# Moving weight sums from VectorE to GpSimd, and two more projections to seven products

## The reference, cut to what matters

```python
proj = x @ w_in[l]                       # 1024 x 6400, cut into 12 pieces:
# a_q 512, a_k 128, a_v 128, b_h 512, b_b 512, b_c 512, c_q 512, c_k 512, c_v 512, g_a, g_b, g_c 1024 each
y_a = sliding_window_attention(a_q, a_k, a_v, sinks)   # 8 heads of 64, 2 key/value heads, window 128
y_b = b_b * conv3(b_c * b_h)
y_c = moba_attention(c_q, c_k, c_v)      # 8 heads of 64; with one block of 256 it is causal attention
merged = sigmoid(g_a)*(y_a @ w_br_a) + sigmoid(g_b)*(y_b @ w_br_b) + sigmoid(g_c)*(y_c @ w_br_c)
x = layer_norm(ALPHA*x + merged @ w_out)
x = layer_norm(ALPHA*x + (silu(x @ w_gate) * (x @ w_up)) @ w_down)    # hidden width 2816
```

## Time and profile before

| | |
|---|---|
| median of 3 runs | 2504.95 us |
| profiled execution | 2509.21 us |
| its span, first to last instruction | 2507.3 us |
| TensorE busy | 2206.5 us, 88% |
| VectorE busy | 1181.2 us, 47% |
| ScalarE busy | 366.2 us, 15% |
| GpSimd busy | 38.5 us, 2% |
| mean granted TensorE clock | 0.96 |

### The profile page before, as it was taken

How to read it: one execution, slowest core, us unless ns; L and a number is a source line. 1 busy time by engine, 2 the same in 40 slices (tenths; PEclk the granted TensorE clock), 3 DMA queues, 4 the chain that set the end, 5 groups by cost and what they waited for, 6 DMA issues and landing times.

```text
span 2507.3 us, 43433 instructions
## 1 busy us (share of the span) xinstructions
PE 2206.5 (88%) x19414; PEld 1567.8 (63%) x19414; DVE 1181.2 (47%) x2135; ACT 366.2 (15%) x818; POOL 38.5 (2%) x69
## 2 busy tenths in 40 slices
PE   8999999999999999999999988888799986555564
PEld 7898699488987984746545645454488643232322
DVE  6776477687755875935533221222435631111111
ACT  1121000012210000234521000000201520000000
POOL 0000000000000010000000000000000000000000
PEclk9999999999999999999998999999999998888877
DMA  8655755476558564511327999999921189999996
GB/s 318 223 167 200 242 183 213 154 252 236 168 185 268 169 222 162 199 45 36 118 111 331 418 427 426 426 427 425 377 103 34 71 339 425 427 426 428 427 427 282
DMA packets 168411, 659.15 MB, mean 263 GB/s; under 512 B 8326, under 2 KB 55938, under 8 KB 143522
## 3 DMA queue, kind: packets, MB, share of 16 engines
q1 hardware_dynamic: 162544, 639.66, 65.5%
q0 software_dynamic: 5312, 16.57, 2.1%
q10 hardware_dynamic: 370, 0.15, 0.0%
HBM read 655.12 MB, written 1.23 MB: 262 GB/s over the span
## 4 chain that ended last, share of the span: by engine, by line
PE 61%; DMA 29%; DVE 7%; ACT 2%; issue 1%; DVEq 0%; SPq 0%; ACTq 0%
PE psum L2291 21%; DMA ring<-in_moe_w_up 10%; DMA ring<-in_moe_w_gate 9%; DMA ring<-in_moe_w_down 9%; PE psum L789 5%; PE psum L2459 4%; PE psum L538 4%; PE psum L2236 3%; PE psum L2349 3%; PE psum L715 3%; PE psum L603 2%; PE psum L601 2%; PE psum L806 2%; PE psum L2467 1%; PE psum L2312 1%; PE psum L859 1%
## 5 line engine op out<-in xcount | busy, mean ns | idle before, releaser
L789 PE MATMUL psum<-ring,arena 128*32 128x256 f32 x5888 | 382.7, 416 | 161.8 <-DMA ring<-in_moe_w_up 87.3
L789 PEld LDWEIGHTS psum<-ring,arena 128*32 128x32 f32 x5888 | 207.8, 118 | 333.5 <-issue 138.3
L806 PE MATMUL psum<-ring,lnp 128*32 128x256 f32 x3072 | 193.9, 407 | 71.0 <-DMA ring<-in_moe_w_down 66.5
L1649 DVE TENSOR_TENSOR arena<-psum,spare 32x512 f32<-32x512 f32 (+1 forms) x128 | 70.9, 554 | 363.5 <-PE psum L806 362.2
L806 PEld LDWEIGHTS psum<-ring,lnp 128*32 128x32 f32 x3072 | 104.3, 116 | 158.4 <-DMA ring<-in_moe_w_down 50.5
L1638 DVE TENSOR_TENSOR lnp<-arena,psum 128x512 f32<-128x512 f32 (+1 forms) x32 | 26.1, 815 | 331.3 <-PE psum L789 331.3
L2291 PE MATMUL psum<-ht,ring 128*128 128x128 f32 x1408 | 168.2, 279 | 4.4 <-DMA ring<-in_w_in 3.4
L2291 PEld LDWEIGHTS psum<-ht,ring 128*128 128x128 f32 x1408 | 163.3, 195 | 8.4 <-issue 8.4
L538 PE MATMUL psum<-ring,ht 128*128 128x512 f32 x320 | 140.6, 595 | 0.0
L1096 ACT ACTIVATE arena<-psum 128x512 f32<-128x512 f32 (+1 forms) x32 | 15.7, 490 | 674.0 <-PE psum L789 674.0
L2693 DVE SCALAR_TENSOR_TENSOR spare<-ring,arena,spare 128x512 f32<-128x512 f32 x168 | 113.4, 743 | 0.0
(11 more groups left out here) (517 smaller groups left out, 3175.0 us busy)
## 6 DMA issues: line engine op xcount, KB each, us to landing
ring<-in_moe_w_down SPq DMA_DIRECT2D x64, 2048.0 KB
ring<-in_moe_w_gate SPq DMA_DIRECT2D x62, 2048.0 KB
ring<-in_moe_w_up SPq DMA_DIRECT2D x60, 2048.0 KB
ring<-in_w_in SPq DMA_DIRECT2D x52, 1024.0 KB
ring<-in_ada_w SPq DMA_DIRECT2D x48, 1024.0 KB
ring<-in_w_ffn_gate SPq DMA_DIRECT2D x22, 1024.0 KB
ring<-in_w_ffn_up SPq DMA_DIRECT2D x22, 1024.0 KB
ring<-in_w_ffn_down SPq DMA_DIRECT2D x20, 1024.0 KB
```

The lines of the kernel that those rows point to most:

```text
L789: last = mm(bank[32 * j:32 * j + 32, SPLIT * m:SPLIT * m + SPLIT], (x_last if layer else x_four)[:, k, e % 4, SLOTS * m:SLOTS * m + SLOTS] ...
L806: last = mm(bank[32 * j:32 * j + 32, SPLIT * m:SPLIT * m + SPLIT], hidT[:, e % 2, a:a + 32], slot[:, f % 4, SPLIT * j:SPLIT * j + SPLIT], ...
L1649: ins = TTo(y_four[32 * q:32 * q + 32, s0:, cols], view(bank[r, 0:width], len(src), SPLIT), gb_moe[r, s0:, cols], ALU.mult)
```

## The change

GpSimd makes the weight sums of every seven-product panel but the first of each layer; VectorE keeps that first one (`first_weight_sums`). The wait is as before, for product 3 of the panel before; the first feed-forward panel waits for the merged branches, and the first ga panel for a transpose of attention a as before. The sums count on a semaphore of their own. GpSimd's loads of ln1 now stand behind the bias rows, both behind the sums of the first 13 panels, and the stores of modulation rows behind the sums of all panels.

The query of attention a (`aq`) and the value of attention c (`cv`) become seven-product panels, so that a layer has 24 instead of 22. The value is wanted with tokens on the partitions, so its products swap the sides and have 256 moving columns, 4 matmuls each. The query comes out with heads in another order; neighbouring heads of a's scores now lie on different halves of the partitions, as c's do, and ScalarE keeps a second copy of the keys with the halves swapped. VectorE's and ScalarE's lists change to match; `ada_sums(0)` is done in two halves around `parts(2)`, `ada_sums(2)` as 3 and 5 eighths in place of 4 and 4.

```diff
-FIRST = {"b": 0, "cq": 3, "ck": 4, "gb": 5, "ga": 7, "gc": 9, "ff": 11}
+FIRST = {"b": 0, "aq": 3, "cq": 4, "ck": 5, "cv": 6, "gb": 7, "ga": 9, "gc": 11, "ff": 13}
-RUNS = (0, 3, 5, 7, 9, 11)
+RUNS = (0, 4, 7, 9, 11, 13)
...
+                def weight_sums(q):          # on GpSimd
+                    n_panel = SEVEN_PANELS[q]
+                    pool.wait_ge(panel_in[n_panel % RING], l * (32 * LAYER_PANELS // RING) + 32 * (n_panel // RING + 1))
+                    if q == FIRST["ff"]:
+                        pool.wait_ge(merged_ready, l + 1)
+                    elif q == FIRST["ga"]:
+                        pool.wait_ge(pe_done, banks.full("layer", ("pta", 7), l))
+                    else:
+                        pool.wait_ge(pe_done, banks.full("layer", ("sv", q - 1, "A"), l) + 1)
...
+                    add(s1, a21, a22, ALU.add).then_inc(pool_sums_ready, 1)
+                    pool.wait_ge(pool_sums_ready, at + 1)
+                    add(s2, s1, a11, ALU.subtract).then_inc(pool_sums_ready, 1)
+                    pool.wait_ge(pool_sums_ready, at + 2)
+                    add(s4, a12, s2, ALU.subtract).then_inc(pool_sums_ready, 1)
+                    add(a21, a11, a21, ALU.subtract).then_inc(pool_sums_ready, 1)
+                for q in range(1, FIRST["ff"]):
+                    weight_sums(q)
                 pool.wait_ge(probs_ready["c"], l + 1)
...
+                pool.wait_ge(pe_done, banks.full("layer", ("sv", FIRST["ff"] - 1, "D"), l))
+                (loads of ln1_g, ln1_b, gain_ffn)
+                for q in range(FIRST["ff"], SEVENS):
+                    weight_sums(q)
                 pool.wait_ge(ada_b_ready, 4 * l + 4)
...
+                            for k in range(4 if q == FIRST["cv"] else 0):
+                                left, right = factor_pair(q, c, k, 0, slot)
+                                last = mm(view(bank[:, SEQ * j:SEQ * j + SEQ], 2, P), right, left, start=k == 0, stop=k == 3)
...
+                seven_products(FIRST["aq"])
-                slot = panel(l, HALF)
-                for m in range(2):
-                    (128 matmuls of the query, 64 weight columns each)
...
-                scores("a", lambda h: aq[64 * (h // 4):64 * (h // 4) + 64, h % 4, :],
-                       lambda h: ak[64 * (h // 4):64 * (h // 4) + 64, :])
+                scores("a", lambda h: aq[64 * (h % 2):64 * (h % 2) + 64, h // 2, :],
+                       lambda h: (ak if h // 4 == h % 2 else ak_swapped)[64 * (h % 2):64 * (h % 2) + 64, :])
...
-                project([("cv", 0), ("cv", 1)], panel(l, HALF), xT)
+                seven_products(FIRST["cv"])
...   (VectorE's list, from panel 1 on)
-                weight_sums(1)
                 parts(0)
-                weight_sums(2)
                 parts(1)
-                ada_sums(0, 0, KT)
+                ada_sums(0, 0, 4)
                 parts(2)
-                weight_sums(3)
+                ada_sums(0, 4, KT)
+                parts(FIRST["aq"])
                 (convolution, logits of a)
                 ada_sums(1, 0, 4)
-                weight_sums(4)
-                parts(3)
+                parts(FIRST["cq"])
                 ada_sums(1, 4, KT)
+                parts(FIRST["ck"])
                 (exponentials' sums, normalise a)
-                parts(4)
-                weight_sums(5)
+                parts(FIRST["cv"])
                 (logits of c)
-                ada_sums(2, 0, 4)
-                weight_sums(6)
-                parts(5)
-                ada_sums(2, 4, KT)
-                parts(6)
+                ada_sums(2, 0, 3)
+                parts(FIRST["gb"])
+                ada_sums(2, 3, KT)
+                parts(FIRST["gb"] + 1)
```

More of the change, by code:

```diff
@@ L2174, in _ @@
                     pool.dma_start(const[:, 128:904], K["const"][:, 128:904]).then_inc(const_rest_loaded, 16)
[L2175 to L2178, removed]
+                def weight_sums(q):
[7 more added lines that the diff above has]
+                        pool.wait_ge(pe_done, banks.full("layer", ("sv", q - 1, "A"), l) + 1)
+                    w = view(ring[:, n_panel % RING, :], KT, 2, 2, P)
+                    a11, a21, a12, a22 = (w[:, 4 * c:4 * c + 4, :, r, :] for c in range(2) for r in range(2))
+                    made = left_sums(q)
+                    s1, s2, s4 = made[5], made[6], made[3]
+                    at = 4 * (l * (SEVENS - 1) + q - 1)
+                    add = nc.gpsimd.tensor_tensor
+                    add(s1, a21, a22, ALU.add).then_inc(pool_sums_ready, 1)
[6 more added lines that the diff above has]
+                    weight_sums(q)
                 pool.wait_ge(probs_ready["c"], l + 1)
@@ L2393, in _ @@
                 seven_products(FIRST["gc"] + 1)
-                wait_emptied(pe, "layer", ("cv", 0), l)
-                wait_emptied(pe, "layer", ("cv", 1), l)
+                for name in "ABCD":
+                    wait_emptied(pe, "layer", ("sv", FIRST["cv"], name), l)
                 attend_values("c", lambda r, g: 2 * r + g, zc, cv, lambda h: 64 * h)
@@ L2539, in _ @@
                 first_product(2)
-                for m in range(2):
-                    take(("aq", m), aq[:, 2 * m:2 * m + 2, :])
-                take(("ak",), ak, part=SEQ)
+                first_product(FIRST["aq"])
+                bank, freed = full_bank(act, "layer", ("ak",), l)
+                A(ak, bank[:, 0:SEQ], ACT.Copy)
+                for g in range(2):
+                    last = A(ak_swapped[64 * g:64 * g + 64, :], bank[64 - 64 * g:128 - 64 * g, 0:SEQ], ACT.Copy)
+                last.then_inc(freed, 1)
                 take(("av",), av, part=SEQ)
-                first_product(3)
+                first_product(FIRST["cq"])
                 exps("a", za).then_inc(exp_ready["a"], 1)
@@ L2583, in _ @@
                 for p in range(PAIRS):
+                    if p == 7:
+                        take(("adaG",), ada_g, part=SEQ)
                     first_product(FIRST["ff"] + p)
@@ L2924, in _ @@
                 for p in range(PAIRS):
[L2925 to L2927 removed]
+                    if p + 1 == PAIRS:
                         turned(0, 8)
```

131 lines of the change are left out of this document (60 added, 71 removed).

## The result

The changed kernel takes 2546.12 us (median of 4 runs, 2545.14 to 2549.85), the kernel before 2504.14 us beside it (4 runs): ratio 1.0163, 95% interval 1.0148 to 1.0178. It is slower by 42 us. My forecast was 2518 with a range to 2544. The direction was right; the time lies at the rival that I gave 0.12, full exclusion (2544).

A forecast was written before the change was run, and what follows sets the result against it. TensorE's own work was taken to bound the first block. Over two layers, -7.4 products, +8.4 tight pairs and +12 contention gave +13: 2518 us from a median of 2505, own range 2510 to 2534, 8 in 10 2496 to 2544.

The forecast's parts named there:

- full exclusion: Rival: GpSimd sums and two-operand VectorE instructions take turns throughout, 38 us more in two layers, 2544 us; chance 0.12.
- query product: Attention a's query on TensorE: in seven products 12.50 us instead of 13.97, 1.47 won per layer.
- value product: Attention c's value on TensorE: seven products take 12.2 us instead of 13.93, 1.7 won per layer.
- scores of a, without contention: New head order cuts a's eight heads from 4.9 to 2.9 us; late bank emptying leaves 1.6 won per layer.
- banks at scores of c: Behind the value product, c's heads wait for banks; next panel starts 4.0 us behind instead of 2.9, 1.1 lost per layer.
- six tight pairs, sums alone: Where the panel before begins with its C bank, four GpSimd sums overrun: 0.7 us a pair, 4.2 per layer.
- contention: pairs: GpSimd sums sharing SBUF with two-operand VectorE instructions make the tight pairs later: 3 us per layer.
- contention: scores of a, modulation rows: VectorE slowed beside GpSimd sums delivers query parts and second modulation group late: 3 us per layer for both waits.
- The price of a sum: One GpSimd sum of 128x1024 takes 2.3 us, between bounds of 1.22 and 2.45.
- the rival of a shorter sum: GpSimd sums below 2.15 us cost nothing at the tight pairs, TensorE's 7.4 us saving stays: 2498 us; chance 0.20.
- my second bound: In contention, each instruction waits out the whole of the other engine's: 19 us per layer, 38 in two.
- The feed-forward stage: Panels of the feed-forward stage stay at 12.50 us with no new wait, four GpSimd sums being covered.

The follow-up runs named there:

- experiment 9: Changed kernel, all sums on VectorE, first gb set behind c's logits, second before first gb parts, third modulation group's accumulations moved later: 2501.98 us against 2506.89 for the kernel before.
- experiment 1: Changed kernel with the modulation accumulations replaced by a one-input maximum over the same weights: 2515.27 us against 2507.39 for the kernel before, ratio 1.0032.
- experiment 3: Changed kernel with all 24 sets of weight sums on VectorE, query and value still in seven products: 2508.55 us against 2507.39 for the kernel before, ratio 1.0004.
- experiment 7: Changed kernel with only the first gb panel's set of sums on GpSimd, all others on VectorE: 2504.16 us against 2506.66 for the kernel before, ratio 0.9987.
- experiment 2: Kernel before with all weight sums but each layer's first moved to GpSimd, query, value and scores unchanged: 2538.14 us against 2507.39, ratio 1.0128.
- experiment 8: As experiment 6, with the sums of feed-forward panels 2 to 10 of a layer on GpSimd: 2509.55 us against 2506.66 for the kernel before, ratio 1.0007.
- experiment 6: Changed kernel with all sums on VectorE and the first gb panel's set behind c's logits: 2509.76 us against 2506.66 for the kernel before, ratio 1.0013.
- experiment 5: Kernel before with only the new query head order and swapped copy of keys, eight products kept: 2501.62 us against 2506.66, ratio 0.9978.

## Why the prediction was wrong in its size

Layer 1, my steps against the traces:

| step | predicted | measured |
|---|---|---|
| query product | -1.47 | -1.5 (12.50) |
| value product | -1.7 | -1.6 at full clock (12.28 in experiment 9); 13.44 here, see the last row |
| scores of a, without contention | -1.6 | -1.3 (3.6 in experiment 1) |
| banks at scores of c | +1.1 | +1.3 (4.23) |
| six tight pairs, sums alone | +4.2 | +6.3 (experiment 1: 0.86 to 1.23 each, product 5 of the pair's second panel to its product 1, 7.15 before) |
| contention: pairs | +3 | +1.4 (7.7 in all) |
| contention: scores of a, modulation rows | +3 for both | +5.7 (9.3 from the start of the scores to the next panel, 3.6 in experiment 1) and +5.7 |
| slower clock behind the two waits | not in the sum | +1.5, +0.5 and +1.2 |

The predicted column sums to 6.5, half of my +13. The measured one sums to about 19, of which 1.0 is the sixth pair, in the feed-forward stage; the 18.1 before it and 1.0 that this execution had lost before its second panel make, but for 0.2, the 18.9 at the output projection. Set against my terms, the products were 0.5 us per layer off, the pairs by themselves 2.1, and contention with the clock behind it, 15.9 where I had 6, was 10 off.

**The products** were right, in size and place. Those of the value and the query bring what I said as soon as nothing waits; experiment 3 shows that with all sums on VectorE something does.

**The price of a sum** was right: 2.36 alone for 2.3 taken, 184 rows, and there is no bound of 1.22 (the rival of a shorter sum fell).

**The tight pairs** were where I put them, in all six. Their size was low, by small amounts that add up over six pairs. I had counted the fourth sum 0.8 late and then took 0.7. In the ck pair of experiment 1 the four sums take 9.5 (87.47 to 97.01) in place of 9.4, and product 7 starts 0.97 late; behind the wait its 16 instructions take 2.05 in place of 1.95, which makes 1.08.

**The failed step is in "Contention": "I take a third, nearer to the low end because VectorE loses 21 sets of 4.9 us per layer and has room behind most delays".** It gave 3 us per layer to the pairs and 3 to the two hand-overs. The runs showed 1.4 and 11.4. The exclusion is complete, as at my second bound, and the share that I took of it rested on a mean over the layer. The load that VectorE lost lay elsewhere; the two groups of eight accumulations stand right before a hand-over to TensorE, and GpSimd is busy through most of both (all but 59.59 to 61.32 and 71.96 to 73.17 of the first, all but the last 1.9 us of the second). At the bound the query's parts reached the scores "some 5 us late": they start at 73.41, where product 4 of the query ends at 68.15, and the wait is 4.3 + 0.5. The modulation rows I had at 9 late at the bound; measured 5.6, since the accumulations begin earlier against TensorE (2.9 us behind the start of ck, 4.5 before) and TensorE itself had lost 1.5 in the pair.

At the bound I also let each GpSimd sum grow by 0.7. Beside accumulations it grows by 0.31 to 0.45, once in each layer by 0.57, less than one accumulation, while the accumulation takes a whole sum. Hence the pairs suffered less than at the bound (1.4 for 5.1) and VectorE's groups the whole. GpSimd isn't spared: its wait is short here because an accumulation is. Beside the normalising of 128x2048 in experiment 7 a sum takes up to 4.40.

The Trainium skill, SBUF — State Buffer, section Who interferes with whom, has VectorE's second port pair and GpSimd's as one under an exclusive lock. The trace and experiment 1 agree: 2.76 us per accumulation with two SBUF inputs, 0.60 with one, 0.41 with one input in PSUM. I had quoted that rule and weighed it at 0.12, because no row could bear on it; nothing spoke for a third.

**The agreement with full exclusion is partly luck.** That rival had 38 us of contention in two layers and none for the clock; doubled, layer 1 shows 32 with the clock's 6 in it. Its 8.4 for the pairs alone were 12.5, and its -7.4 for the products were -6.2. The errors offset each other.

**The clock** was in none of my cases. In the 4 to 6 us in which TensorE waits, the granted clock falls (0.79 over the wait below), and stays at 1.2 GHz (0.50) for the first 4 us of the next work. The windows of the changed kernel around the wait at a's scores (stretch, length, busy times of TensorE, its weight loads, VectorE, ScalarE and GpSimd, granted clock as a share of 2.4 GHz, DMA share, GB/s):

```profile
72.00:78.00 6.00, 5.49 (x57) 4.86 (x58) 5.71 (x14) 1.34 (x4) 0.00 (x0) 1.00 0.83 275
78.70:83.50 4.80, 0.57 (x5) 0.17 (x2) 4.73 (x11) 0.00 (x0) 0.00 (x0) 0.79 1.05 398
83.50:87.50 4.00, 3.95 (x15) 3.30 (x16) 3.87 (x8) 0.00 (x0) 0.00 (x0) 0.50 1.05 387
```

The first 32 products behind it take 5.36 in place of 3.84, and the value's first 16 behind the other wait 4.88 in place of 3.72. Together with the 0.5 of the modulation rows that is 3.1 us per layer, on top of 11.4 at the two hand-overs themselves.

**The layer's end** had a wait that my sum left out, 1.1 us for the modulation vector (L2896), in the first layer alone. It is not in experiment 2 and is in experiment 3, so it belongs to the new products and lists, not to GpSimd; which line of the list moves it was not tried.

**The feed-forward stage** was right: 12.50 us per panel behind the first pair, no new wait, and experiment 8. So were the moved DMAs: GpSimd's store of the modulation rows begins at 444.2, my 425 and the 19 that the layer is late, and no wait of TensorE hangs on it.

## What to carry to other kernels

Before moving additions to GpSimd, list VectorE's instructions with two SBUF inputs that would run beside them: each of these can wait out one whole GpSimd instruction, however short it is itself (0.17 became 2.37, 0.68 became 2.76), and a GpSimd instruction in turn one of VectorE's. What counts is whether a hand-over to TensorE stands behind a row of them. Move sums into stretches where VectorE reads PSUM or one operand, or where each has a whole panel's slack, and keep tight sums where the fast engine is. Waits of TensorE of 2.6 to 5.6 us cost another 1.2 to 1.7 us here by the slower clock behind them (experiment 6: 0.66 over the 4 us behind a wait of 2.6). Work saved on TensorE is a gain only after the next hand-over has been followed through.

## What the runs showed of the hardware

- Two-input SBUF additions of 128x1024: 2.36 us on GpSimd, 1.22 on VectorE; of 128x512: 1.26 and 0.69. Beside accumulations GpSimd's become 2.7 to 2.9 and 1.6, some 0.3 to 0.6 more at either length; beside VectorE's normalising of 128x2048 up to 4.40 (experiment 7).
- Beside back-to-back sums of 128x1024 VectorE gets one 0.68 us accumulation per 2.76 us.
- Matmuls that use 64 rows of the array run closer together when neighbours use different halves: eight heads in 2.93 us in place of 4.89, with the same number of instructions (experiment 5). This is the one that I had counted on.
- Of one profiled execution the second block varies by up to 5.7 us by itself, more than several of the effects here; the start of that block was the better mark.
